# Staggering two block inversions by half a level, and making a retention head's decay tables before the heads start

## The reference

```python
gamma = jnp.exp(jnp.where(tril, g[..., :, None] - g[..., None, :], -jnp.inf))
lower = jnp.where(strict, jnp.einsum('bhnid,bhnjd->bhnij', kb, k) * gamma, 0.0)
tmat = lower + jnp.eye(C, dtype=lower.dtype)
solve = lambda rhs: lax.linalg.triangular_solve(tmat, rhs, left_side=True, lower=True, unit_diagonal=True)
u = solve(v * beta[..., None]);  w = solve(kb * jnp.exp(g)[..., None])
...
dec = jnp.exp(jnp.where(tril, (pos[:, None] - pos[None, :]) * lg[:, :, None], -jnp.inf))
o_inner = jnp.einsum('bhnij,bhnje->bhnie', jnp.einsum('bhnid,bhnjd->bhnij', q, k) * dec[:, None], v)
```

## Time and profile before

| what | us |
|---|---|
| median of 3 runs | 2118.88 (2118.25 to 2120.61) |
| the profiled execution, and its span | 2122.73, span 2121.1 |
| PE busy | 2034.9 (96% of the span) |
| DVE, ACT, POOL busy | 1305.3, 753.2, 112.2 |
| chain that ended last: PE, DVE, ACT, "issue" | 86%, 7%, 3%, 2% |

### The profile page before, as it was taken

How to read it: one execution, slowest core, us unless ns; L and a number is a source line. 1 busy time by engine, 2 the same in 40 slices (tenths; PEclk the granted TensorE clock), 3 DMA queues, 4 the chain that set the end, 5 groups by cost and what they waited for, 6 DMA issues and landing times.

```text
span 2121.1 us, 28323 instructions
## 1 busy us (share of the span) xinstructions
PE 2034.9 (96%) x10463; PEld 1721.3 (81%) x10463; DVE 1305.3 (62%) x1861; ACT 753.2 (36%) x966; POOL 112.2 (5%) x173
## 2 busy tenths in 40 slices
PE   9999999998998799999999999999999999898998
PEld 7888888885887788888888888888886788787886
DVE  6877678747537676777578753453355434666666
ACT  4322222316435334332222343212232126745453
POOL 1000001000002120000001000000000000100000
PEclk8999999999998999999999999999999999999999
DMA  8455555431110002455455432342233224133553
GB/s 338 162 190 179 176 195 175 153 110 40 60 50 19 1 1 99 163 189 176 168 197 169 168 119 94 116 167 98 65 115 104 95 82 149 47 119 139 179 198 119
DMA packets 52651, 274.94 MB, mean 130 GB/s; under 512 B 6128, under 2 KB 7472, under 8 KB 34256
## 3 DMA queue, kind: packets, MB, share of 16 engines
q1 hardware_dynamic: 33024, 203.97, 27.6%
q0 software_dynamic: 18960, 69.01, 9.9%
q10 hardware_dynamic: 576, 0.69, 0.1%
HBM read 272.60 MB, written 1.05 MB: 129 GB/s over the span
## 4 chain that ended last, share of the span: by engine, by line
PE 86%; DVE 7%; ACT 3%; issue 2%; DMA 1%; SPq 0%; POOL 0%; DVEq 0%; ACTq 0%
PE ps L1019 16%; PE ps L1021 16%; PE ps L1020 16%; PE ps L1031 8%; PE ps L1246 5%; PE ps L1244 5%; PE ps L1245 5%; PE ps L1032 4%; DMA ada<-in_ada 1%; ACT w_hi L472 1%; DVE w_lo L690 1%; PE ps L2346 1%; PE ps L1873 1%; PE ps L1869 1%; PE ps L1186 1%
## 5 line engine op out<-in xcount | busy, mean ns | idle before, releaser
L1019 PE MATMUL ps<-h_parts,w_lo 128*128 128x512 f32 (+1 forms) x1592 | 608.3, 382 | 5.9 <-DVE h_parts L811 4.4
L1021 PE MATMUL ps<-h_parts,w_hi 128*128 128x512 f32 (+1 forms) x1592 | 602.3, 378 | 0.0
L1020 PE MATMUL ps<-h_parts,w_hi 128*128 128x512 f32 (+1 forms) x1592 | 602.2, 378 | 0.0
L472 ACT ACTIVATE w_hi<-w_raw 128x2048 fp32r<-128x2048 f32 (+3 forms) x207 | 353.9, 1710 | 500.5 <-PE ps L1246 254.0
L690 DVE TENSOR_TENSOR w_lo<-w_raw,w_hi 128x2048 fp32r<-128x2048 f32 (+3 forms) x207 | 422.0, 2039 | 135.9 <-ACT w_hi L472 135.4
L1019 PEld LDWEIGHTS ps<-h_parts,w_lo 128*128 128x128 f32 x1592 | 302.2, 190 | 63.8 <-DVE w_lo L690 5.0
L1020 PEld LDWEIGHTS ps<-h_parts,w_hi 128*128 128x128 f32 x1592 | 302.1, 190 | 55.8 <-issue 1.4
L1021 PEld LDWEIGHTS ps<-h_parts,w_hi 128*128 128x128 f32 x1592 | 301.9, 190 | 55.6
L698 DVE SCALAR_TENSOR_TENSOR ada_product<-ada_w,silu_c 128x1024 bf16<-128x1024 f32 x256 | 313.1, 1223 | 20.3 <-DVE ada_product L698 9.8
L484 ACT ACTIVATE sil<-ps 128x512 f32<-128x512 f32 x66 | 39.5, 598 | 480.6 <-PE ps L1021 480.6
L1031 PE MATMUL ps<-h_parts,w_hi 128*128 128x512 f32 x544 | 195.7, 403 | 5.7 <-DVE h_parts L895 2.5
(11 more groups left out here) (327 smaller groups left out, 2240.5 us busy)
## 6 DMA issues: line engine op xcount, KB each, us to landing
w_raw<-in_w_up SPq DMA_DIRECT2D x88, 1024.0 KB, 4.8
ada_w<-in_ada POOLq DMA_DIRECT2D x128, 512.0 KB, 3.6
w_raw<-in_w_down SPq DMA_DIRECT2D x32, 768.0 KB, 4.2
w_raw<-in_w_ret SPq DMA_DIRECT2D x24, 1024.0 KB, 4.8
w_raw<-in_w_down SPq DMA_DIRECT2D x32, 640.0 KB, 3.9
w_raw<-in_w_ab SPq DMA_DIRECT2D x14, 1024.0 KB, 4.8
ada<-in_ada SPq DMA_DIRECT2D x8, 1024.0 KB, 27.0
w_raw<-in_w_ret_out SPq DMA_DIRECT2D x8, 1024.0 KB, 4.8
```

Source lines behind the costliest of these rows:

```text
L472: act.activation(w_hi[parts_of(s, slot)][:, 0:elems], w_raw[slot][:, 0:elems], ACT.Copy).then_inc(hi_ready, 1)
L1019: pe.matmul(out, lo, rhs_hi(k), start=first and k == 0, stop=False)
L1020: pe.matmul(out, hi, rhs_lo(k), start=False, stop=False)
L1021: mm = pe.matmul(out, hi, rhs_hi(k), start=False, stop=last and k == nk - 1)
```

## The change

Four things in the inversions. (1) PE makes the decay sums of both chunks first, then the key products, then the query products. (2) The order of the levels is staggered: PE runs X(0,l), the corrections of chunk 1 of level l-1, the corrections of chunk 0 of level l, X(1,l); ACT goes chunk by chunk. (3) POOL writes the level-1 cut to `xbuf`, so that it waits for the coupling only ("SYS"), and the level-2 cut waits for "T0". (4) DVE starts chunk 0's level 0 before it ends chunk 1's coupling. In the scan of s = 1 one KS product stands ahead of chunk 1's last correction. In the retention, head 0's tables are made at other places: ACT's exponentials before the gate's steps, DVE's join after the gate's second step, POOL's copy of the keys as soon as they are there; the buffers for it move to the memory of `silu_c`, which is free by then.

```diff
-    r_decay = [put(f"r_decay{i}", [P, 6 * P], at=at_h + 4 * KB * i)[0] for i in range(2)]
+    r_decay = [put(f"r_decay{i}", [P, 6 * P], at=(at_ada + 8 * KB, at_h)[i])[0] for i in range(2)]
...
     def pool_deltanet(pool):
-                    if l == 1:
-                        inv(pool, iv_dve, INV_DVE, c, s, "T0")
+                    if l < 3:
+                        inv(pool, iv_dve, INV_DVE, c, s, ("SYS", "T0")[l - 1])
                     else:
                         inv(pool, iv_pe, INV_PE, c, s, f"X{l - 1}")
-                    pool.tensor_tensor(cut[c][:], coup[c][:], over(levels[:, l * P:(l + 1) * P], 4), ALU.mult) \
+                    pool.tensor_tensor((xb if l == 1 else cut)[c][:], coup[c][:], over(levels[:, l * P:(l + 1) * P], 4), ALU.mult) \
...
     def pe_invert(pe, s):
+        turn(0)
+        cross(0, 1)
+        turn(1)
+        correct(0, 1)
+        cross(1, 1)
+        for l in range(2, LEVELS):
+            cross(0, l)
+            correct(1, l - 1)
+            correct(0, l)
+            cross(1, l)
+        if s == 1:
+            pe_scan_keys(pe, s, 0, 0)
+        correct(1, LEVELS - 1)
...
     def act_deltanet(act):
                     act.activation(parted(heads(turned[c]), l), crossed(trn[c], l), ACT.Copy).then_inc(iv_act[c], 1)
-                for c in range(2):
                     inv(act, iv_pe, INV_PE, c, s, f"X{l}")
                     act.activation(heads(xb[c]), bank(0, c), ACT.Copy).then_inc(iv_act[c], 1)
...
     def dve_invert(dve, s):
+        joined(0)
+        coupled(0)
+        joined(1)
+        begun(0)
+        coupled(1)
+        begun(1)
...
     def pool_retention(pool):
         pool.wait_ge(rroped, 8)
+        stage(0, 0)
         pool.wait_ge(step_done, S_RG + 8)
+        stage(1, 1)
+        pool.wait_ge(r_scores, 2)
...
     def act_ret(act):
-        walk(act, "retg", g_body)
         act.wait_ge(decays_ready, 1)
         act.wait_ge(tables_ready, 16)
+        decays(0, 0)
+        walk(act, "retg", g_body)
...
     def dve_ret(dve):  # g_body
             if ahead:
                 split_lo(dve, s + 2, slot, ahead)
+            if isinstance(r, int) and r == 1:
+                join_decays(0, 0)
```

More of the change, by code:

```diff
@@ L1839, in pe_invert, with turn @@
             mm.then_inc(iv_pe[c], 1)
[L1840 to L1849, removed]
-        for c in range(2):
+        for w in (1, 0):
+            for c in range(2):
+                tt = slice((2 * s + c) * P, (2 * s + c + 1) * P)
+                if w == 0 and c == 1 and s == 0:
+                    pe.wait_ge(g_read, 1)
+                for h in range(DNH):
+                    mm = pe.matmul(bank(3 - w, c)[:, h * P:(h + 1) * P], dn[:, 1, h, tt], dn[:, w, h, tt],
+                                   start=True, stop=True)
+                mm.then_inc(iv_pe[c], 1)
+        def turn(c):
             inv(pe, iv_act, INV_ACT, c, s, "EG")
@@ L1855, in pe_invert, with cross @@
             mm.then_inc(iv_pe[c], 1)
[L1856 to L1859, removed]
-                inv(pe, iv_pool, INV_POOL, c, s, f"M{l}")
+        def cross(c, l):
+            inv(pe, iv_act, INV_ACT, c, s, "FILL")
+            inv(pe, iv_dve, INV_DVE, c, s, f"N{l - 1}")
+            inv(pe, iv_pool, INV_POOL, c, s, f"M{l}")
+            for h in range(DNH):
+                mm = pe.matmul(bank(0, c)[:, h * P:(h + 1) * P], (xb if l == 1 else cut)[c][:, h, :],
+                               crossed(nrm[c], l, h), start=True, stop=True)
+            mm.then_inc(iv_pe[c], 1)
@@ new lines, in pe_invert, with pe_scan_keys @@
+        turn(0)
[8 more added lines that the diff above has]
+            cross(1, l)
+        if s == 1:
+            pe_scan_keys(pe, s, 0, 0)
+        correct(1, LEVELS - 1)
+    def pe_scan_keys(pe, s, b, d):
+        c = chunk(d, s, b) % 2
+        scan(pe, st_dve, ST_DVE, d, f"ST{(2 * s + b - 1) // 2}{(b + 1) % 2}")
+        inv(pe, iv_dve, INV_DVE, c, s, "KE")
+        for h in range(DNH):
+            mm = pe.matmul(bank(0, d)[:, h * P:(h + 1) * P], eg[c][:, d, h, :], state[d][:, h, :],
+                           start=True, stop=True)
+        mm.then_inc(st_pe[d], 1)
@@ L1879, in pe_scan @@
         before = f"{(2 * s + b - 1) // 2}{(b + 1) % 2}"
+        if not first(s, b):
+            for d in range(2):
+                if not (b == 0 and d == 0):
+                    pe_scan_keys(pe, s, b, d)
         if b == 0:
@@ L1883, in pe_scan @@
         if not first(s, b):
-            for d in range(2):
-                c = chunk(d, s, b) % 2
-                scan(pe, st_dve, ST_DVE, d, "ST" + before)
-                inv(pe, iv_dve, INV_DVE, c, s, "KE")
-                for h in range(DNH):
-                    mm = pe.matmul(bank(0, d)[:, h * P:(h + 1) * P], eg[c][:, d, h, :], state[d][:, h, :],
-                                   start=True, stop=True)
-                mm.then_inc(st_pe[d], 1)
             for d in range(2):
@@ L1984, in dve_invert, with joined @@
             op.then_inc(iv_dve[c], 1)
-        for c in range(2):
+        def joined(c):
             tt = 2 * s + c
@@ L1999, in dve_invert, with begun @@
             dve.tensor_tensor(cut[c][:], coup[c][:], over(levels[:, 0:P], 4), ALU.mult).then_inc(iv_dve[c], 1)
-        for c in range(2):
+        def begun(c):
             inv(dve, iv_pe, INV_PE, c, s, "X0")
@@ L2512, in body @@
             if has(1):
-                dec, back = r_decay[1 - b], r_back[1 - b]
-                dve.wait_ge(r_exps, h + 2)
-                dve.tensor_tensor(dec[:, 384:768], dec[:, 384:768], back[:, 384:768], ALU.mult).then_inc(r_halves, 1)
-                dve.tensor_tensor(dec[:, 0:384], dec[:, 0:384], back[:, 0:384], ALU.add)
-                dve.wait_ge(r_halves, h + 2)
-                dve.tensor_tensor(dec[:, 512:640], dec[:, 512:640], ident, ALU.add).then_inc(r_decayed, 1)
+                dec = r_decay[1 - b]
+                if not (isinstance(h, int) and h == -1):
+                    join_decays(h + 1, 1 - b)
                 dve.wait_ge(r_decayed, h + 2)
```

62 lines of the change are left out of this document (32 added, 30 removed).

## The result

The changed kernel takes 2100.56 us (median of 4 runs, 2098.14 to 2101.47) beside 2119.74 for the kernel before on the same chip: ratio 0.9903, interval 0.9887 to 0.9918. The direction was right and so was nearly every step. The start of a superchunk gives 1.9 us more than I gave it. Some 2.5 us more lie where the change edits nothing; the ratio's interval, 17.4 to 23.9 us on 2118.88, holds the 18.0 us that the changed stages show.

What follows compares the result with a forecast made beforehand. PE, busy 96% of the span, was taken as the bound, so only its waits and low-clock stretches could give time. Inversions 10.2 plus retention 6.0 make 16.2 us: 2118.88 to 2102.7, range 2099.5 to 2109.

Steps and rivals of the forecast that it cites:

- Start of a superchunk: Inversions, up to chunk 0's level 2: decay sums first and earlier crossed product gain 4.7 us each, between 2.2 and 5.1.
- the meeting with POOL: Start of a superchunk: POOL's early cut and DVE delay each other in SBUF, priced at 1.3 us, ends 0 and 2.6.
- the 0.4 that I held back for the corrections: Start of a superchunk: level 2 was reckoned at 737.1 with the clock back at 734.7, but taken as 737.5.
- rival 1: Start: low clock lasts to level 2 despite PE's earlier restart; 2.5 us less per superchunk, 2107.7; 15 in 100.
- rival 2: Start and levels 2 and 3: POOL's cuts precede DVE's instructions on the path; 6.2 us lost in all, 2108.9; 12 in 100.
- Levels: Levels 2 to 6: staggering cuts 24.69 us to 21.9 per superchunk, gain 2.8, between 1.0 and 3.3.
- the 0.06 us of slack: Levels: a reply takes 1.72 us while PE has 1.78 us of other groups, so PE need not wait.
- the 0.4 us reserved for its failing: Inversions: 10.2 us kept instead of 10.6 for two superchunks, as PE's slack in the levels will sometimes not do.
- Rival 4: Levels: clock stays low through whole levels, 7.0 us more each; 2130.7 if two levels per superchunk; 3 in 100.
- End: End of a superchunk: last subtraction comes 6.4 us after chunk 0's level-6 product instead of 4.18, loss 2.2 each.
- Retention: Head 0's earlier tables gain 6.0 us: 3.1 from the mix starting sooner, 2.9 from it running at full clock.
- Rival 3: Retention: the clock falls anyway, or only the wait is gained; 3.1 us instead of 6.0, 2105.6; 10 in 100.

Runs made afterwards that it cites:

- e10: The kernel before with the whole new start (sums, DVE's order, POOL's early cut) but the old level order and retention: ratio 0.9984, 1.49 us gained in the inversion stages.
- e11: The changed kernel with chunk 1's first crossed product put ahead of chunk 0's level-1 corrections: 2.54 and 3.09 us slower in superchunks 0 and 1; ratio to before 0.9935.
- e6: The kernel before with only the staggered level order of PE and ACT, old start and retention: ratio 0.9982, 1.64 us gained in the inversion stages.
- e7: The kernel before with only both chunks' decay sums moved ahead of the key and query products: ratio 0.9989, 1.67 us gained in the inversion stages.
- e5: The changed kernel with POOL's level-1 cut back in `cut`, waiting for "T0": 4.83 us slower than the changed kernel in the stages; ratio to before 0.9940.
- e12: The changed kernel with DVE's old order at the start and the KS product back in the scan: stages 0.84 and 2.03 us longer; ratio to before 0.9922.
- e8: The kernel before with 16 unread products filling PE's idle time ahead of head 0's mix: retention stage 2.80 us shorter; ratio 0.9991, interval including 1.
- e1: The changed kernel with the old retention, so only the inversions changed: ratio to the kernel before 0.9931, 12.18 us gained in the inversion stages.
- e3: The whole changed kernel measured once more against the kernel before: ratio 0.9914, 18.13 us gained in the stages.

## Why the prediction was right and where it was wrong

**Start of a superchunk: the step that failed, in its size.** Predicted 4.7 each, between 2.2 and 5.1; measured 5.97 in superchunk 1 and 5.31 in superchunk 0, both above that range, so 1.9 us more in all. Three things were mis-sized in superchunk 1. The first crossed product came 4.18 nearer to the sums (3.8 predicted): the meeting with POOL cost 1.1 instead of 1.3, on another instruction, and the rest is small gaps. The clock was back 3.1 us after PE's restart, not 4.1, so the corrections took 1.19 and 1.06 instead of starting with a slow group. And the 0.4 that I held back for the corrections wasn't needed. In superchunk 0 the first product came 3.97 nearer (11.38 after the first exponent, for 15.35), and the rest, 1.3, was gained behind it, although both corrections were slow (1.91 and 1.38): before, two products at 2.05 and a correction at 1.68 stood there. So rival 1 (2107.7), that the clock stays low to level 2, didn't come in either. That it could have come close is shown by e10 (low to 735.0, level 2 at 736.96) and e11 (low to 728.3, level 2 at 729.33), with the same early restart. My argument against rival 1 ("the work is no less dense") was too loose: what decided was that chunk 0's corrections, which wait for nobody, came before a product that waits.

The same way of reckoning missed for the parts (e6, e7 and e10: 0.6, 2.6 and 6.0 expected; 1.64, 1.67 and 1.49 measured). In e7 and e10 the first product came as early as reckoned, and what failed was the time for which the clock stays low behind it, the term that was off in the prediction too, there to the other side. No run here gave a way to tell that time beforehand. That the whole change came as near as it did is in that sense partly luck.

**POOL.** It didn't come first (rival 2): DVE's `cut` stayed ahead of it. Its cuts of chunk 1 cost PE at most 0.24 us in a level (level 3, ahead of the correction at 737.98). That the early cut was needed at all, e5 shows: 4.8 us.

**Levels.** Predicted 21.9, measured 21.97 and 21.95, a gain of 2.7 each. PE goes from group to group with gaps of no more than 0.24 us, 0.15 in the mean of a level (21.97 / 4 is 5.49, for 5.34 of work), which the 0.5 in the sum nearly covers. So the 0.06 us of slack held, and the 0.4 us reserved for its failing (in all) was not needed. Rival 4 didn't come.

**End.** Predicted 6.4 behind chunk 0's level-6 product, measured 6.58 and 6.57: the loss is 2.4, not 2.2. KS fills a hole and buys nothing, as said (e12).

**Retention.** Predicted 6.0, measured 5.96, with the two parts as split: DVE's weighing right behind L690 (1791.97; 1789.76 + 2.29 - 0.09 = 1791.96), the mix 1.34 later, and 2.8 to 2.9 of clock, isolated by e8. The clock's part holds against profiles of before whose mix took 6.57; that the one I priced from was among the slowest (5.12 to 6.57) is luck. Rival 3 didn't come. Nothing added in the gate can be seen in PE's time there: "rest" is 1015.81 to 1016.64 in the changed kernel and 1016.78 in e1, which has the old gate.

**Sum.** By stages 18.0 instead of 16.2. The start gave 1.9 more; what levels and end fell short by (0.5) and the reserve that wasn't needed (0.4) cancel. And 2118.88 - 18.0 = 2100.8 would have been inside the range (e3's ratio gives 2100.7). The last 2.5 us of the first ratio are not in the stages. They are the opening and the rest, or chance of the measurement, and for these the range had no room: between profiles of one kernel the opening alone moves by 3 us, which one profile of before could not show, but the spread of the three given times (2.4 us) hinted at.

## What to carry to other kernels

When several streams restart together after idle time, put first on PE what waits for nobody: one group that waits 1.2 us between the restart and the dense work cost 2.5 to 3 us here, about half of it because the clock stayed low behind it. Parts of a reordering that lie on one chain are worth little one by one (1.5, 1.6, 1.7) and much together (12.1), so price the chain as a whole and don't reject the idea on a part. An engine that is late for one chunk is late for the other too, and for what stands behind in its queue (POOL in e5); list both before moving an instruction.
